# Streaming encoder layer on one core: three RMS norms with the tokens on the partitions

## The reference

```
def rmsnorm(x, g):
    y = xf * lax.rsqrt(jnp.mean(xf * xf, axis=-1, keepdims=True) + EPS)
    return (y * g.astype(jnp.float32)).astype(x.dtype)

h = modulate(rmsnorm(x, ln1), sh1, sc1)        # before the input projection
x = x + g1 * (concat(retention, attention) @ w_out)
h2 = modulate(rmsnorm(x, ln2), sh2, sc2)       # before the gated MLP
x = x + g2 * ffn
y = modulate(rmsnorm(x, norm_f), shf, scf)     # the output
```

## Time and profile before

| | us |
|---|---|
| median of 3 runs (lowest, highest) | 1325.32 (1324.27, 1325.89) |
| the profiled execution, its own time | 1324.34 |
| its span in the trace | 1322.5 |
| PE busy | 1254.9 (95%) |
| DVE busy | 840.2 (64%) |
| ACT busy | 517.5 (39%) |
| POOL busy | 520.5 (39%) |

### The profile page before, as it was taken

How to read it: one execution, slowest core, us unless ns; L and a number is a source line. 1 busy time by engine, 2 the same in 40 slices (tenths; PEclk the granted TensorE clock), 3 DMA queues, 4 the chain that set the end, 5 groups by cost and what they waited for, 6 DMA issues and landing times.

```text
span 1322.5 us, 22445 instructions
## 1 busy us (share of the span) xinstructions
PE 1254.9 (95%) x8537; PEld 1182.0 (89%) x8537; DVE 840.2 (64%) x1503; ACT 517.5 (39%) x1029; POOL 520.5 (39%) x313
## 2 busy tenths in 40 slices
PE   5999999999999999779999999999999999999995
PEld 3568988988989899779999999999999999999995
DVE  6988477396496637995666666666665468663305
ACT  4454345344345513543333333433333323333422
POOL 0012131031232514544353534435352577775760
PEclk9999999999999899899999999999999999999998
DMA  9413032222233412103223232222322898686971
GB/s 363 177 58 125 25 121 79 81 80 87 74 112 103 149 60 99 58 32 132 99 100 115 92 124 99 100 99 100 115 94 83 324 367 289 238 310 213 332 258 46
DMA packets 74392, 185.55 MB, mean 140 GB/s; under 512 B 7424, under 2 KB 39744, under 8 KB 74048
## 3 DMA queue, kind: packets, MB, share of 16 engines
q1 hardware_dynamic: 72640, 183.63, 38.9%
q10 hardware_dynamic: 1664, 0.72, 0.2%
HBM read 150.14 MB, written 34.19 MB: 139 GB/s over the span
## 4 chain that ended last, share of the span: by engine, by line
PE 68%; DVE 12%; POOL 6%; issue 5%; DMA 5%; ACT 2%; SPq 1%; DVEq 0%; ACTq 0%; POOLq 0%
PE bank L2189 33%; PE bank L1922 14%; PE bank L2229 9%; PE bank L2165 5%; DMA w_raw<-in_w_units 3%; POOL w_extra L1315 2%; POOL w_more L1315 2%; PE bank L2036 2%; DVE std L1559 1%; PE bank L2006 1%; PE bank L2021 1%; DVE ada_out L1352 1%; DVE act_hl L1406 1%; POOL w_hl L1315 1%; POOL w_hl L1276 1%
## 5 line engine op out<-in xcount | busy, mean ns | idle before, releaser
L1922 PE MATMUL bank<-act_hl,w_hl 128*128 128x362 f32 (+1 forms) x1368 | 256.5, 336 | 1.3 <-DVE act_hl L1406 1.3
L1922 PEld LDWEIGHTS bank<-act_hl,w_hl 128*128 128x128 f32 x1368 | 223.3, 188 | 10.6 <-issue 8.3
L1203 POOL TENSOR_TENSOR w_hl<-w_raw,w_hl 128x1024 fp32r<-128x1024 f32 x21 | 51.3, 2444 | 332.5 <-ACT w_hl L730 332.5
L2229 PE MATMUL bank<-u_hl,w_more 128*128 128x362 f32 (+1 forms) x672 | 116.3, 332 | 2.6 <-POOL w_more L1315 2.3
L2189 PE MATMUL bank<-x_blocks_a,w_hl 128*128 128x272 f32 x864 | 114.0, 291 | 4.9 <-issue 4.9
L2229 PEld LDWEIGHTS bank<-u_hl,w_more 128*128 128x128 f32 x672 | 113.5, 191 | 3.3 <-POOL w_more L1315 2.6
L2189 PEld LDWEIGHTS bank<-x_blocks_a,w_hl 128*128 128x128 f32 x864 | 111.6, 191 | 5.3 <-issue 5.1
L2189 PE MATMUL bank<-x_blocks_a,w_ext 128*128 128x272 f32 x840 | 110.1, 290 | 4.3 <-DVE prod_sb L1664 2.4
L2189 PE MATMUL bank<-x_blocks_b,w_hl 128*128 128x272 f32 x864 | 112.7, 288 | 1.6 <-ACT x_blocks_b L1013 1.3
L2189 PEld LDWEIGHTS bank<-x_blocks_b,w_hl 128*128 128x128 f32 x864 | 109.8, 188 | 2.4 <-DVE up_b L1669 1.3
L2189 PEld LDWEIGHTS bank<-x_blocks_a,w_ext 128*128 128x128 f32 x840 | 107.5, 190 | 5.0 <-issue 2.6
(11 more groups left out here) (233 smaller groups left out, 2277.7 us busy)
## 6 DMA issues: line engine op xcount, KB each, us to landing
w_raw<-in_w_units SPq DMA_DIRECT2D x139, 512.0 KB, 4.5
ada_w<-in_w_ada_t SPq DMA_DIRECT2D x36, 512.0 KB, 3.6
u_hl<-u_dram SPq DMA_DIRECT2D x44, 362.0 KB, 5.5
u_dram<-acc SPq DMA_DIRECT2D x22, 544.0 KB, 2.7
u_dram<-up_b SPq DMA_DIRECT2D x22, 544.0 KB, 2.7
ada_d<-in_w_ada_t SPq DMA_DIRECT2D x16, 512.0 KB, 5.7
u_hl<-u_dram SPq DMA_DIRECT2D x22, 364.0 KB, 7.3
xm<-in_x_t SPq DMA_DIRECT2D x2, 1448.0 KB, 13.8
```

The costliest lines, as they stand in the source:

```text
L1203: pool.tensor_tensor(w_hl[:, slot, 1], w_raw[:, slot], w_hl[:, slot, 0].bitcast(F32), ALU.subtract).then_inc(wl_ready, 1)
L1922: ins = pe.matmul(bank[c][:, 0:m], w_hl[:, slot, w, k, :], act_hl[:, x, k, a:a + m], start=(pas == 0 and i == 0), stop=(pas == 2 and i == ...
L2229: ins = pe.matmul(bank[o][:, 0:m], w_down(q)[:, w, o, :], u_hl[:, q % U_RING, x, 0:m], start=(f == pas == 0), stop=(f == FT - 1 and pas == 2))
```

## The change

The operands of the summing matmuls trade places. Each 128x128 block of squares (or of `acc`) becomes the stationary operand, and one column of ones streams past. The result is one column with a token on each partition, so 362 tokens are three columns (`token_groups`: blocks that start at 0, 128 and n-128, the last two overlapping). Root and reciprocal then work on 128x3 elements. To bring the reciprocal back to all partitions, PE transposes each column, read as a 128x128 block by repeating it, which gives 128 tokens along the free axis on all partitions (`spread_inverse`).

The spread result lies in PSUM. In the first stage ACT copies it to `std` (`x_copy_inverse`). In the output projection and in the last chunk DVE reads it from PSUM; for POOL in the last chunk PE makes a second copy in another bank and ACT copies that to SBUF. The identity matrix is loaded ahead of the conditioning tiles in the first stage, and again in the two later stages, where its place has been reused. The first two chunks of the last norm stay as they were.

```diff
         X_SQ = [sq[:, 0], sq[:, 1], hf[:, 0], hf[:, 1]]
-        X_SUM_BANK = [4, 5, 6]
+        X_SUM_BANK = [3, 4, 5]
+        ident_o, std_o, inv_o = gate_w[:, 0:P], gate_w[:, P:P + 12], gate_w[:, P + 12:P + 24]
...
             sp.dma_start(silu_c[:, :, :], cond.partition_broadcast(P)).then_inc(cond_loaded, 16)
+            sp.dma_start(ident[:], ident_in).then_inc(ident_loaded, 16)
...
+            sp.wait_ge(state_stored, 32 * HEADS + 32)
+            sp.dma_start(ident_o, ident_in).then_inc(ident_o_loaded, 16)
...
+                if q == 10:
+                    sp.dma_start(ident_d[:, :], ident_in).then_inc(ident_d_loaded, 16)
...
             def x_root(c):
-                act.activation(std_flat[:, CHUNKS[c][0]:sum(CHUNKS[c])], bank[X_SUM_BANK[c]][:, 0:n], ACT.Sqrt, bias=eps_sb[:, 0:1],
+                act.activation(std_x[:, 3 * c:3 * c + 3], bank[X_SUM_BANK[c]][:, 0:3], ACT.Sqrt, bias=eps_sb[:, 0:1],
                                scale=1.0 / D).then_inc(std_ready, 1)
+            def x_copy_inverse(c):
+                act.wait_ge(x_spread, c + 1)
+                act.activation(std_flat[:, a:a + n], bank[X_SUM_BANK[c]][:, 8:8 + n], ACT.Copy).then_inc(x_inverse, 1)
...
-            x_squares(0)
-            x_root(0)
-            x_squares(1)
-            x_root(1)
-            x_squares(2)
-            x_root(2)
+            act.activation(sqrt_eps[:, :], eps_sb[:, :], ACT.Sqrt)
+            x_squares(0, range(KT))
+            x_squares(1, range(KT))
+            x_root(0)
+            x_squares(2, range(4))
+            x_root(1)
+            x_copy_inverse(0)
+            x_squares(2, range(4, KT))
+            x_copy_inverse(1)
+            x_root(2)
+            x_copy_inverse(2)
...
             def scale_x(*steps):
                 for i in steps:
+                    dve.wait_ge(x_inverse, sum(a < hi for a, _ in CHUNKS))
...
             def x_sums(c):
                 for k in range(KT):
-                    ins = pe.matmul(bank[X_SUM_BANK[c]][:, 0:n], ones[:, :], X_SQ[item % 4][:, 0:n], start=(k == 0),
-                                    stop=(k == KT - 1))
+                    for g, o in enumerate(token_groups(CHUNKS[c][1])):
+                        ins = pe.matmul(at[:, g:g + 1], X_SQ[item % 4][:, o:o + P], ones[:, 0:1], start=(k == g == 0),
+                                        stop=(k == KT - 1), skip_group_check=True)
                     ins.then_inc(sq_used, 1)
+            def spread_inverse(at, inv, groups, ident_at):
+                for g, o in enumerate(groups):
+                    ins = pe.transpose(at[:, o:o + P], inv[:, g:g + 1].broadcast_to([P, P]), ident_at)
+                return ins
             x_sums(0)
             x_sums(1)
+            x_spread_inverse(0)
             x_sums(2)
+            x_spread_inverse(1)
+            x_spread_inverse(2)
...
-            pe.wait_ge(std_ready, 3)
+            pe.wait_ge(x_inverse, 3)
...
                 if r == 26:
+                    pe.wait_ge(x_normed2, 1)
                     out_total(2)
+                if r == 27:
+                    out_spread_inverse(2)
```

More of the change, by code:

```diff
@@ L248, in hymba_step @@
         ident_loaded = sem("ident_loaded")
+        ident_o_loaded = sem("ident_o_loaded")
+        ident_d_loaded = sem("ident_d_loaded")
+        x_inverted = sem("x_inverted")
+        x_spread = sem("x_spread")
+        x_inverse = sem("x_inverse")
+        out_inverted = sem("out_inverted")
+        out_spread = sem("out_spread")
+        final_inverted = sem("final_inverted")
+        final_spread = sem("final_spread")
+        final_inverse = sem("final_inverse")
         w_loaded = [sem(f"w_loaded{slot}") for slot in range(3)]
@@ L551, in _ @@
                 sp.dma_start(dst[:], src).then_inc(const_loaded, 16)
-            sp.dma_start(ident[:], ident_in).then_inc(ident_loaded, 16)
             load_first_ada(6)
@@ L764, in _, with x_squares @@
             act.wait_ge(pool_const, 2)
-            def x_squares(c):
+            def x_squares(c, ks):
                 a, n = CHUNKS[c]
                 act.wait_ge(x_loaded[c], 16)
-                for k in range(KT):
+                for k in ks:
                     item = KT * c + k
@@ L1153, in final_root, with copy_final_inverse @@
                 act.wait_ge(fsum_ready, c + 1)
[L1154 to L1155 removed]
+                to, at = (std[:, c, 0:n], bank[7][:, 0:n]) if c < 2 else (std_d[:, :], bank[0][:, 0:3])
+                act.activation(to, at, ACT.Sqrt, bias=eps_sb[:, 0:1], scale=1.0 / D).then_inc(fstd_ready, 1)
+            def copy_final_inverse():
+                n = CHUNKS[2][1]
+                act.wait_ge(final_spread, 2)
+                act.activation(std[:, 2, 0:n], bank[1][:, 0:n], ACT.Copy).then_inc(final_inverse, 1)
             def final_modulate(c, k):
@@ L1388, in first_invert @@
             def first_invert(c):
-                at = std_flat[:, CHUNKS[c][0]:sum(CHUNKS[c])]
                 dve.wait_ge(std_ready, c + 1)
-                then_wait(dve.reciprocal(at, at))
+                dve.reciprocal(inv_x[:, 3 * c:3 * c + 3], std_x[:, 3 * c:3 * c + 3]).then_inc(x_inverted, 1)
             def scale_x(*steps):
@@ L1412, in _ @@
             first_invert(0)
-            for m in (5, 6):
-                first_ada_dots(m)
+            first_ada_dots(5)
             first_invert(1)
+            first_ada_dots(6)
             first_vectors(0)
@@ L1890, in _ @@
                 final_add(2, k - 1)
-            final_invert(2)
+            dve.wait_ge(fstd_ready, 3)
+            dve.reciprocal(inv_d[:, :], std_d[:, :]).then_inc(final_inverted, 1)
             final_scale(2, 2)
@@ L2144, in out_total, with out_spread_inverse @@
                 pe.wait_ge(out_add, {0: 12, 1: 13, 2: 24, 3: 27}[n] + 1)
-                pe.matmul(bank[OUT_SUM_BANK[n]][:, 0:HC], ones[:, :], acc[:, HC * n:HC * n + HC], start=True,
-                          stop=True).then_inc(out_sum, 1)
+                for g, o in enumerate(token_groups(HC)):
+                    ins = pe.matmul(bank[OUT_SUM_BANK[n]][:, HC + g:HC + g + 1], acc[:, HC * n + o:HC * n + o + P],
+                                    ones[:, 0:1], start=True, stop=True)
+                ins.then_inc(out_sum, 1)
+            def out_spread_inverse(n):
+                pe.wait_ge(ident_o_loaded, 16)
+                pe.wait_ge(out_inverted, n + 1)
+                spread_inverse(bank[OUT_SUM_BANK[n]][:, 0:HC], inv_o[:, 3 * n:3 * n + 3], token_groups(HC),
+                               ident_o).then_inc(out_spread, 1)
             for r, (o, n) in enumerate(OUT_JOBS):
@@ L2262, in _ @@
             pe.wait_ge(down_evac, 16 + 8)
-            pe.matmul(bank[0][:, 0:m], ones[:, :], acc[:, a:a + m], start=True, stop=False)
+            groups = token_groups(m)
+            for g, o in enumerate(groups):
+                pe.matmul(bank[0][:, g:g + 1], acc[:, a + o:a + o + P], ones[:, 0:1], start=(g == 0), stop=False,
+                          skip_group_check=True)
             pe.wait_ge(fsq_ready, 16 + 8)
-            pe.matmul(bank[0][:, 0:m], ones[:, :], sq[:, 1, 0:m], start=False, stop=True).then_inc(fsum_ready, 1)
+            for g, o in enumerate(groups):
+                ins = pe.matmul(bank[0][:, g:g + 1], sq[:, 1, o:o + P], ones[:, 0:1], start=False, stop=True,
+                                skip_group_check=True)
+            ins.then_inc(fsum_ready, 1)
+            pe.wait_ge(ident_d_loaded, 16)
+            pe.wait_ge(final_inverted, 1)
+            spread_inverse(bank[0][:, 8:8 + m], inv_d, groups, ident_d[:, :]).then_inc(final_spread, 1)
+            spread_inverse(bank[1][:, 0:m], inv_d, groups, ident_d[:, :]).then_inc(final_spread, 1)
 MIX_ORDER = [4, 5, 6, 7, 0, 1, 2, 3]
```

70 lines of the change are left out of this document (46 added, 24 removed).

## The result

The changed kernel takes 1333.16 us in the median of four runs (1332.43 to 1335.27), the kernel before 1325.61 in the same comparison: ratio 1.0058, interval 1.0042 to 1.0074. The forecast was 1331.6 in a range of 1316.3 to 1334.0, slower at 0.48; the measured time lies 0.8 us under the upper end of that range. The profiled execution took 1333.17, with a span of 1331.4, and is set beside the 1324.34 of before: +8.8.

The account below looks back on a forecast made before the run. PE, busy 95%, was taken as the bound, so norms cost time only at the start, around the output projection's end and in the last chunk. Forecast: 1324.34 + 11.6 - 2.8 - 1.5 = 1331.6 us, range 1316.3 to 1334.0.

Parts of the forecast that it names:

- Price of a sum: Summing one tile on PE takes six loads: 1.28 us at half clock, taken for the first stage, or 0.66 at full.
- the first rival: First stage: loads stay at 0.11 us, as the clock rises or doesn't matter; stage -1.5, total 1318.5, chance 0.38.
- First stage: Start of the kernel up to the unit loop: sums at 1.28 us a tile delay it by 11.6 us.
- the spare time ahead of the unit loop: First stage: PE has 1.7 us to spare before the unit loop, taken off a delay of 13.3 us.
- Output projection: Stage after the heads: nothing gained to job 24, then DVE saves, -2.8 us in sum (-5 to -1).
- root 3: Output projection, from job 25: this root stands behind a modulation on ACT, costing 0.3 us.
- job 27's wait: Output projection: job 27 stands on PE behind quarter 2's total and spread, so DVE idles 2.7 us.
- the low parts of x: Output projection: DVE's low parts of x now fall beside POOL's work, costing 1.1 us.
- The additions and the two reciprocals: Output projection, from job 25, on DVE: additions to acc save 1.6 us, two shorter reciprocals 3.4 us.
- Last chunk: End of the kernel: shorter sums, root and reciprocal; ACT becomes last, 1.5 us sooner (-1 to -2.2).
- the slower rival: Output projection: DVE stands 5 us instead of 2.7, leaving that stage about 0; total 1334.4, chance 0.05.
- The case in between: First stage: about 1.0 us a tile, 0.165 a load; stage +5, total 1325.0, no change, chance 0.14.

Follow-up runs that it names:

- ones_128_columns: Changed kernel with every load kept, but first-stage sums streaming 128 columns of ones instead of one: 1319.01 us, 0.9950 of the kernel before.
- first_stage_alone: Kernel before with only the first stage changed, output projection and last chunk as they were: 1339.44 us, 1.0102 of the kernel before.
- first_as_before: Changed kernel with the first stage restored to that of the kernel before: 1319.38 us, 0.9948 of the kernel before.
- warm_start: Changed kernel, single columns kept, with eight matmuls of 512 columns on PE ahead of the first square: 1333.21 us, 1.0051 of the kernel before.

## Why the prediction was right

**Price of a sum.** Forecast 1.28 us a tile at half clock, measured 1.28. That it fits to the hundredth is luck: 6 x 0.21 is 1.26, and two rows gave the 0.21. The choice of half clock ("since the squares no longer stream anything") is what the runs confirm. Both reasons of the first rival fell: the clock did not rise on the sums, and a load does depend on it; it takes 0.11 at full clock (0.74 us for six in the last chunk) and 0.21 at half. So the rule of the Trainium skill, *TensorE: Matmul & The Clock Gate*, "LDWEIGHTS (loading the stationary operand)", P / 1.2 ns, holds at the upper level alone; the measurement decides. With the clock up, in ones_128_columns, the total is 1319.0 where that rival said 1318.5, which is luck in part: its first stage came at +0.9 and not -1.5, since the first tiles still ran at half clock, and its last chunk at -0.7 and not -1.5.

**First stage.** Forecast +11.6, measured +12.4 (98.66 - 86.22), and 13.5 by the ratio of first_stage_alone. The path is right in each step: root 0 at 29.86 (29.5), reciprocals at 30.14 and 35.26 (29.75 and 34.8), second copy done at 47.3 (46.3), first product at 51.56 (50.7). Two small terms make up the 0.8. The first square came 0.2 late and a chunk of sums took 10.5 and 10.7 us for the 10.24 of eight tiles, short pauses at its ends included, so that the second spread began at 45.89 and not at 45.0; from the second copy to the first product it was then 4.3 us for the 4.4 forecast. The products made up half of this. The other term is the spare time ahead of the unit loop: I had 1.7 us, but PE's nine transpositions at 83.81 stand there too, and PE's pause in the earlier trace rows is 1.27.

**Output projection.** Forecast -2.8, by the marks -3.45 in the changed kernel, -2.86 alone, and -3.7 in the mean of all profiles. The size is near, but by terms that cancel. From the last addition ahead of total 2 to `f = 0`'s second evacuation DVE took 26.56 us before (536.85 to 563.41) and 23.05 after (549.53 to 572.58). Too small were the waits: DVE idles 2.48 and 2.32 us, 4.8 in all, where 2.7 was forecast, and 1.04 behind root 3 for 0.3. I had priced job 27's wait without the clock, which falls around the pause of 2.72 us ahead of total 2 and makes job 26 5.44 us. Too dear were the low parts of x: forecast 1.1 us slower, they got 0.9 faster in sum. And one saving had no term at all: DVE's modulation of quarter 3, 3.88 us before, takes 2.00. The additions and the two reciprocals are near the forecast (-1.3 and -3.6 there, for -1.6 and -3.4). For the additions the Trainium skill, *SBUF — State Buffer*, "Who interferes with whom", names the reason (two SBUF inputs against a GpSimd instruction that reads SBUF). The trace agrees in 570 against 771 ns, and more plainly in single ones: 0.43 us with POOL idle, 2.78 at 517.85 of the kernel before, where a tensor_tensor of POOL starts at 517.78. No run here tries it by itself.

**Last chunk.** Forecast -1.5, measured -0.1, because every load behind the first six is at half clock. This is the term that failed. It is the same quantity as in the first stage, and I had used its full-clock price here with no reason but that PE had been busy until then. Where the clock was up, ACT started 1.4 us sooner, and from the first sum to the end of the span it is 13.4 us for 14.7 (first_as_before): the size was right in that condition. Even there it is right by terms that offset each other: the forecast had ACT start 1.0 us sooner (1311.4 for POOL's 1312.42), and the span ends 4.5 us behind ACT's last modulation where it ended 3.9 behind DVE's.

**Sum.** 12.4 - 3.5 - 0.1 = 8.9 for the span, forecast 7.3. Of the slower rival the 5 us of standing for DVE came (4.8), by the clock over job 26 and not by ACT's order, and its consequence did not, since the terms above paid for it. The case in between needed a load of 0.165, which no run shows: a load costs 0.11 or 0.21.

**Open.** Why the modulation and the low parts got faster was read from POOL's rows beside them and not tried; why the clock fell in warm_start; how often it is up in the last chunk; and whether transpositions count for the clock: here they always stood behind single columns, or behind a pause, or behind 128 columns at a clock that was up already (28.20 in ones_128_columns, three in 0.51 us).

## What to carry to other kernels

Swapping stationary and moving operand trades streamed columns for loads, and a matmul of one column costs its load: count loads, and price them at both clock levels. A stretch of loads with single columns to stream ran a whole stage at half clock here though PE read as busy; streaming more columns than are needed, of the same result, let the clock rise and gave 14 us. A sum that waits for another engine can stand behind the next job of its queue: the pause was paid a second time in the job that followed at half clock (5.4 us for 3.2), and moving it gave 2.4 us.

## What the runs showed of the hardware

- PE's load of 128x128 fp32 weights goes with the clock: 0.112 us from load to load at 2.4 GHz (12 in 1.34, ones_128_columns), 0.213 at 1.2 (12 in 2.56, changed kernel).
- A DVE reciprocal takes 2.42 us for 128x364 fp32, 1.85 for 128x272 and 0.18 for 128x3.
- PE busy from 13.64 to 45.6 us in loads and single columns, with pauses of 0.3 us, did not get the clock up. In warm_start, where it was up at the first sum, it fell within two tiles (0.81, then 0.50), behind a pause of 4.08 us, and stayed down. With 128 columns for each load it rose within the fifth tile.
- The granted clock of a window reads 1.00 in the first microseconds though the engine runs at half (24 to 34 us of the changed kernel, loads at 0.21).
- The same code falls or does not fall to half clock in pauses of the same length: the pause of 1.25 us ahead of the last sums was followed by six loads in 0.81 us in some executions, in 1.42 in others; the first stage with 128 columns ended at 84.43, 85.16, 86.90 and 87.13 in four runs that have it alike.
